# Output products of two attentions in one stream, and the query product taken ahead of its normalisation

## What is computed

```
h = rms_norm(x, norm_mix_g)
qa, ka, va, qb, kb, vb, ga, gb = split(h @ w_in)
ya = windowed_attention(qa, ka, va) @ w_oa      # 8 heads of 128
yb = dilated_attention(qb, kb, vb) @ w_ob       # 4 heads of 128
x  = x + (sigmoid(ga) * ya + sigmoid(gb) * yb) @ w_out
h  = rms_norm(x, norm_ffn_g)
q  = h @ peer_wq                                # 16 query parts of 128
top 16 of q . keys for each part, top 16 of the 256 sums, softmax -> gates of experts
x  = x + sum over experts of gate * gelu(h . u) * v
out = rms_norm(x, norm_final_g)
```

## Time and profile before

| | |
|---|---|
| median of 3 runs | 2307.59 us (2306.1 to 2307.99) |
| the profiled execution's own time | 2307.83 us |
| its span, first to last instruction | 2306.0 us |
| mean granted TensorE clock | 0.993 |
| PE busy | 2251.5 us, 98% |
| DVE busy | 1523.8 us, 66% |
| ACT busy | 1054.3 us, 46% |
| POOL busy | 177.3 us, 8% |

### The profile page before, as it was taken

How to read it: one execution, slowest core, us unless ns; L and a number is a source line. 1 busy time by engine, 2 the same in 40 slices (tenths; PEclk the granted TensorE clock), 3 DMA queues, 4 the chain that set the end, 5 groups by cost and what they waited for, 6 DMA issues and landing times.

```text
span 2306.0 us, 40258 instructions
## 1 busy us (share of the span) xinstructions
PE 2251.5 (98%) x12034; PEld 1930.6 (84%) x12034; DVE 1523.8 (66%) x2475; ACT 1054.3 (46%) x1541; POOL 177.3 (8%) x222
## 2 busy tenths in 40 slices
PE   7999999999898999999999999999999999999997
PEld 6888888888687888888888888888888888888885
DVE  6555566676567888878999999555555555555555
ACT  5444455446444444454444444444444444444443
POOL 0000000001302012221111111000000000000000
PEclk9999999999999999999999999999999999999999
DMA  6655544445454555554444444556555656555553
GB/s 223 227 186 183 181 164 156 154 144 204 137 190 171 169 179 182 182 182 164 159 160 162 164 160 159 185 187 215 195 191 192 192 195 212 191 191 193 194 195 137
DMA packets 114690, 415.56 MB, mean 180 GB/s; under 512 B 12974, under 2 KB 15662, under 8 KB 114022
## 3 DMA queue, kind: packets, MB, share of 16 engines
q1 hardware_dynamic: 114662, 415.23, 54.0%
HBM read 410.94 MB, written 4.24 MB: 180 GB/s over the span
## 4 chain that ended last, share of the span: by engine, by line
PE 95%; DVE 2%; ACT 1%; issue 1%; POOL 1%; DMA 0%; POOLq 0%; SPq 0%; DVEq 0%; ACTq 0%
PE ps L1251 40%; PE ps L1476 30%; PE ps L1254 20%; PE ps L1453 2%; PE ps L1362 1%; PE ps L1344 1%; POOL merged L456 1%; DVE lo L756 0%; DMA raw<-w_qk 0%; PE ps L1353 0%; PE ps L1422 0%; ACT hi L499 0%; ACT move L538 0%; DVE y L1238 0%; DVE work L774 0%
## 5 line engine op out<-in xcount | busy, mean ns | idle before, releaser
L1251 PE MATMUL ps<-move,hi 128*128 128x512 f32 x3840 | 1384.0, 403 | 31.2 <-DVE lo L756 18.5
L756 DVE TENSOR_TENSOR lo<-raw,hi 128x1024 fp32r<-128x1024 f32 x760 | 930.6, 1225 | 664.8 <-PE ps L1476 335.1
L1254 PE MATMUL ps<-move,lo 128*128 128x256 f32 x3840 | 1040.6, 281 | 0.0
L499 ACT CAST hi<-raw 128x1024 fp32r<-128x1024 f32 x760 | 791.3, 1047 | 201.4 <-DMA raw<-w_down 108.4
L1251 PEld LDWEIGHTS ps<-move,hi 128*128 128x128 f32 x3840 | 719.2, 189 | 190.5 <-DVE lo L756 17.3
L1254 PEld LDWEIGHTS ps<-move,lo 128*128 128x128 f32 x3840 | 729.4, 190 | 16.3
L507 ACT COPY upper<-ps 128x256 f32<-128x256 f32 x272 | 100.7, 373 | 645.5 <-PE ps L1251 645.3
L1476 PE MATMUL ps<-hi,act_hi 128*128 128x512 f32 x1024 | 315.5, 389 | 1.6 <-DVE lo L756 1.5
L1476 PE MATMUL ps<-lo,act_hi 128*128 128x512 f32 x1024 | 315.2, 389 | 0.0
L1476 PE MATMUL ps<-hi,act_lo 128*128 128x512 f32 x1024 | 315.2, 389 | 0.0
L1476 PEld LDWEIGHTS ps<-hi,act_hi 128*128 128x128 f32 x1024 | 192.0, 188 | 42.3 <-DVE lo L756 1.9
(11 more groups left out here) (162 smaller groups left out, 974.2 us busy)
## 6 DMA issues: line engine op xcount, KB each, us to landing
raw<-w_u SPq DMA_DIRECT2D x256, 512.0 KB, 3.3
raw<-w_down SPq DMA_DIRECT2D x256, 512.0 KB, 3.4
raw<-w_qk SPq DMA_DIRECT2D x68, 512.0 KB, 3.3
raw<-w_gate SPq DMA_DIRECT2D x64, 512.0 KB, 3.3
raw<-w_out SPq DMA_DIRECT2D x32, 512.0 KB, 3.3
raw<-w_pq SPq DMA_DIRECT2D x32, 512.0 KB, 3.6
raw<-w_v SPq DMA_DIRECT2D x28, 512.0 KB, 3.3
raw<-w_oa SPq DMA_DIRECT2D x16, 512.0 KB, 3.3
```

Of the source, the lines that this page charges most:

```text
L499: nc.scalar.copy(hi[slot][:], raw[slot][:]).then_inc(hi_ready, 1)
L756: nc.vector.tensor_tensor(lo[s % LOS][:], raw[s % RAW][:], hi[s % RAW][:].bitcast(F32), ALU.subtract).then_inc(lo_ready, 1)
L1251: return nc.tensor.matmul(ps[bank][:], hi[slot][:, col:col + P], m, start=first, stop=last)
L1254: return nc.tensor.matmul(ps[bank][:, 0:T], lo[lslot][:, col:col + P], m[:, 0:T], start=False, stop=False, skip_group_check=True)
```

## The change

oa and ob become one stage o of 24 chunks in the order a0 b0 a1, b1 a2 a3, b2 a4 a5, ... (`O_ORDER`; the weights are stacked so on the host). In o and pq every weight tile gets three products of 256 columns that accumulate in one place (`added`: high by high, low by high, high by low), so no halves are left to copy and add. DVE's `weigh` takes blocks from PSUM and multiplies by the gates; POOL has no part in it. In out, ACT and DVE also split g * x1, without rstd, into a new buffer `move2` (`keep_raw`, `split_raw`), from which pq is computed. The sum of squares, rstd, the 32 transposes and the split of the normalised h for u move in between pq's chunks (`squares_and_turns`, `norm2`, `root2`, `keep_h2`, `split_h2`, `turned`); POOL multiplies x1 by rstd into `xr` (four instructions of 1024 columns). Since scores now lack rstd, the exponential gets it as a factor per token (`rstd_tok`). ACT copies query blocks from PSUM. The copy of the turned x1 to memory is issued behind pq's loads, and POOL's fill of `act` waits for pq's last chunk. The buffer of turned x1 moves from 64 KB to 32 KB of the arena. The o loops and the pq loops are unrolled.

The diff, cut to what the text speaks of:

```diff
...
-CHUNKS = {"qk": 2 * N_QK, "v": 2 * N_V, "gate": 2 * N_GATE, "oa": KT, "ob": KT // 2,
+CHUNKS = {"qk": 2 * N_QK, "v": 2 * N_V, "gate": 2 * N_GATE, "o": KT + KT // 2,
           "out": 2 * KT, "pq": 2 * HC, "u": 2 * NK, "down": 2 * NK}
-BLOCKS = {"qk": N_QK, "v": N_V, "gate": N_GATE, "oa": KT, "ob": KT, "out": KT, "pq": HC, "u": NK}
+BLOCKS = {"qk": N_QK, "v": N_V, "gate": N_GATE, "o": KT, "out": KT, "pq": HC, "u": NK}
...
+UPPER0 = {"qk": 0, "out": BLOCK0["o"], "u": BLOCK0["o"] + KT}
...
-TURN_BANKS = (2, 3, 4, 6, 7)
+TURN_BANKS = (2, 3, 4)
...
+TURN0 = 2 * BODY
...
+O_ORDER = [("a", 0), ("b", 0), ("a", 1)]
+for _n in range(1, KT // 2):
+    O_ORDER += [("b", _n), ("a", 2 * _n), ("a", 2 * _n + 1)]
+O_DONE = [()] * len(O_ORDER)
+for _c, (_kind, _n) in enumerate(O_ORDER):
+    if _c == 1:
+        O_DONE[_c] = (0,)
+    elif _c > 1 and _kind == "a":
+        O_DONE[_c] = (_n,)
...
-        h2 = at("h2", ARENA + 48 * KB, [P, KT, T])
-        x1_nat = at("x1_nat", ARENA + 64 * KB, [P, TT, D])
+        move2 = at("move2", ARENA + 48 * KB, [P, KT, 2 * T], F32R)
+        xr = at("xr", ARENA, [P, KT, T])
+        x1_nat = at("x1_nat", ARENA + 32 * KB, [P, TT, D])
...
+        rstd_tok = at("rstd_tok", ARENA + 113 * KB + 64, [P, TT])
...
+            with sp.Fori(0, 2) as it:
+                for s in range(BODY):
+                    load("o", it, s)
+            sp.wait_ge(att_ready, 4)
+            sp.dma_start(x_again[:], A["x_t"]).then_inc(x_again_in, 16)
+            with sp.Fori(2, CHUNKS["o"] // BODY) as it:
+                for s in range(BODY):
+                    load("o", it, s)
...
-            sp.wait_ge(merged_lo, KT + 4)
+            sp.wait_ge(merged_lo, KT)
             sp.dma_start(keys_sb[:], A["keys"]).then_inc(keys_in, 16)
-            sp.wait_ge(x1_copied, 8)
-            sp.dma_start(x1_dram.ap(), x1_nat[:].rearrange("p a d -> p (a d)")).then_inc(x1_out, 16)
             with sp.Fori(1, CHUNKS["pq"] // BODY) as it:
                 for s in range(BODY):
                     load("pq", it, s)
+            sp.wait_ge(x1_copied, 8)
+            sp.dma_start(x1_dram.ap(), x1_nat[:].rearrange("p a d -> p (a d)")).then_inc(x1_out, 16)
...
-            pool.wait_ge(gated_a, KT + 2)
-            with pool.Fori(0, KT // 4) as it:
-                for e in range(4):
-                    n = it * 4 + e
-                    pool.wait_ge(block_summed, n + BLOCK0["ob"] + 3)
-                    pool.wait_ge(sig_ready, KT)
-                    nc.gpsimd.tensor_tensor(merged[e][:], merged[e][:], pick1(gates, n + KT), ALU.mult).then_inc(gated_b, 1)
-                    pool.wait_ge(gated_b, n + 1)
-                    nc.gpsimd.tensor_tensor(merged[e][:], merged[e][:], pick1(gates, n), ALU.add).then_inc(merged_ready, 1)
+            pool.wait_ge(x1_ready, KT)
             nc.gpsimd.iota(iota16[:], [[1, TOPK]], base=0, channel_multiplier=0,
                            allow_small_or_imprecise_dtypes=True).then_inc(iota_ready, 1)
-            pool.wait_ge(move_ready, 8)
+            pool.wait_ge(rstd_done, 1)
+            for q in range(4):
+                part = slice(4 * q, 4 * q + 4)
+                nc.gpsimd.tensor_tensor(xr[:, part, :], x1[:, part, :], rstd[:].unsqueeze(1).to_broadcast([P, 4, T]),
+                                        ALU.mult).then_inc(xr_ready, 1)
+            pool.wait_ge(xr_ready, 4)
+            pool.wait_ge(chunk_used, CHUNK0["u"] + RAW)
             pool.wait_ge(x1_out, 16)
...
+                    if name == "pq":
+                        if s % 2:
+                            n, e = it * 2 + s // 2, s // 2
+                            a.wait_ge(chunk_used, it * BODY + c0 + s + 1 + RAW)
+                            a.wait_ge(key_scores, n + 1)
+                            nc.scalar.copy(query[e][:], ps[e][:, 0:T]).then_inc(block_summed, 1)
...
+            def sigmoid_of(n):
+                a.wait_ge(block_summed, BLOCK0["gate"] + KT + n + 3)
+                both = gates[:].rearrange("p (k n) t -> p k n t", k=2)[:, :, n, :]
                 nc.scalar.activation(both, both, ACT.Sigmoid).then_inc(sig_ready, 1)
-            a.wait_ge(block_summed, BLOCK0["gate"] + KT + 2 + 2)
-            gate(0, -2)
-            gate(0, -1)
-            with a.Fori(0, CHUNKS["oa"] // BODY - 1) as it:
-                body("oa", it, gate)
-            body("oa", CHUNKS["oa"] // BODY - 1, lambda it, s: gate(it, s) if s < 2 else None)
-            def keep_merged(it, s):
-                for e in range(2):
-                    n = it * 8 + 2 * s + e
+            def keep_merged(c):
+                for n in O_DONE[c]:
                     a.wait_ge(merged_ready, n + 1)
-                    nc.scalar.copy(move[:, bass.ds(n, 1), 0:T].rearrange("p a t -> p (a t)"), merged[s % 2 * 2 + e][:]
-                                   ).then_inc(merged_hi, 1)
-            left = run(a, body, "ob", (keep_merged, 1), carry=True)
+                    nc.scalar.copy(move[:, n, 0:T], merged[n % 4][:]).then_inc(merged_hi, 1)
+            sigmoid_of(0)
+            sigmoid_of(1)
+            for c in range(CHUNKS["o"]):
+                hi_of(CHUNK0["o"], 0, c + 2)
+                if c + 2 < KT:
+                    sigmoid_of(c + 2)
+                if c >= 2:
+                    keep_merged(c - 2)
+            def last_merged(it, s):
+                keep_merged(CHUNKS["o"] - 2)
+                keep_merged(CHUNKS["o"] - 1)
+            left = [(last_merged, 1, 0)]
...
+            def keep_raw(it, s):
+                if s % 2:
+                    n = it * 2 + s // 2
+                    a.wait_ge(x1_ready, n + 1)
+                    nc.scalar.activation(move2[:, bass.ds(n, 1), 0:T].rearrange("p a t -> p (a t)"), pick1(x1, n), ACT.Copy,
+                                         scale=g_ffn[:, bass.ds(n, 1)]).then_inc(raw_hi, 1)
...
+            def root2(it, s):
+                if it == 0 and s == 2:
+                    nc.scalar.preload_act_table(ACT.Sqrt)
+                if it == 1 and s == 0:
+                    a.wait_ge(inv_ready, 2)
+                    nc.scalar.activation(rstd[:], work[:], ACT.Sqrt).then_inc(root_ready, 1)
+                if it == 2 and s == 2:
+                    a.wait_ge(rstd_turned, 1)
+                    nc.scalar.copy(rstd_tok[:], ps[5][:, 0:T].rearrange("p (t k) -> p t k", t=TT)[:, :, 0]).then_inc(rstd_kept, 1)
+            def keep_h2(it, s):
+                k = it * BODY + s - TURN0
+                if 0 <= k < KT:
+                    a.wait_ge(xr_ready, k // 4 + 1)
+                    nc.scalar.activation(move[:, k, 0:T], xr[:, k, :], ACT.Copy, scale=g_ffn[:, k:k + 1]).then_inc(h2_hi, 1)
...
+            for tt in range(TT):
+                nc.scalar.activation(found_g[:, tt, :], found_g[:, tt, :], ACT.Exp, scale=rstd_tok[:, tt:tt + 1]
+                                     ).then_inc(soft_ready, 1)
...
+            def weigh(c):
+                kind, i = O_ORDER[c]
+                v.wait_ge(chunk_used, CHUNK0["o"] + c + 1 + RAW)
+                if kind == "b":
+                    v.wait_ge(sig_ready, 2 * i + 2)
+                    for n in (2 * i, 2 * i + 1):
+                        nc.vector.tensor_tensor(gates[:, KT + n, :], ps[2 + n % 2][:, 0:T], gates[:, KT + n, :], ALU.mult
+                                                ).then_inc(gated_b, 1)
+                else:
+                    v.wait_ge(sig_ready, i + 1)
+                    nc.vector.tensor_tensor(merged[i % 4][:], ps[i % 2][:, 0:T], gates[:, i, :], ALU.mult
+                                            ).then_inc(block_summed, 1)
+                for n in O_DONE[c]:
+                    v.wait_ge(block_summed, BLOCK0["o"] + n + 3)
+                    v.wait_ge(gated_b, n + 1)
+                    nc.vector.tensor_tensor(merged[n % 4][:], merged[n % 4][:], gates[:, KT + n, :], ALU.add
+                                            ).then_inc(merged_ready, 1)
...
+            def split_merged(c):
+                for n in O_DONE[c]:
                     v.wait_ge(merged_hi, n + 1)
-                    nc.vector.tensor_tensor(move[:, bass.ds(n, 1), T:2 * T].rearrange("p a t -> p (a t)"),
-                                            merged[s % 2 * 2 + e][:],
-                                            move[:, bass.ds(n, 1), 0:T].rearrange("p a t -> p (a t)").bitcast(F32),
-                                            ALU.subtract).then_inc(merged_lo, 1)
-            left = run(v, body, "ob", (gate_b, 1), (split_b, 2), carried=left, carry=True)
+                    nc.vector.tensor_tensor(move[:, n, T:2 * T], merged[n % 4][:], move[:, n, 0:T].bitcast(F32), ALU.subtract
+                                            ).then_inc(merged_lo, 1)
+            for c in range(CHUNKS["o"]):
+                lo_of(CHUNK0["o"], 0, c + 1)
+                if c == 0:
+                    keep_gate(N_GATE // 2, -1)
+                    split_att(3)
+                if c >= 2:
+                    split_merged(c - 2)
```

(106 more changed lines are left out.)

169 lines of the change are left out of this document (41 added, 128 removed).

## The result

The changed kernel takes 2285.48 us (median of 4 runs, 2285.29 to 2286.26) against 2307.79 us (4 runs, 2306.1 to 2308.1): a ratio of 0.9906, interval 0.9892 to 0.992. Run again on another chip it gave 2284.67 us and 0.9902 (0.9885 to 0.9918). The gain is 22.3 us; 27.0 were forecast, with a range of 2274 to 2292 us.

A forecast was written before the change was run, and what follows sets the result against it. PE, busy for 98% of the span, was taken as the bound. Terms of 68.4 + 90.4 + 95.9 + 4.7 + 4.5 = 263.9 us replace 290.9, 27.0 less, so 2307.83 becomes 2280.8 us; range 2274 to 2292.

The forecast's parts named there:

- Rival B: Stream o waits on VectorE: 1.3 us at each of eight b-chunks, 10 us given back, 2291 us; chance 0.08.
- Rival A: VectorE bounds pq: eight blocks with splits each 0.8 us over, norm costing 8 us, 2290.7 us left; chance 0.15.
- Rival C: In `added`, weight loads bound narrow products: 0.57 us a tile instead of 0.353, kernel at 2378 us; chance 0.03.
- Rival D: No change in kernel time: several small delays together eat the 27 us; chance 0.03.
- Step (b): Three products of 256 columns instead of 512 + 256 per tile: zero, upper end 3 us, twice that for rounded rows.
- The start of o: First chunks of stream o: 0.7 us on top of 24 chunks at 2.82 us, 68.4 us in all.
- Step (g): In pq, norm and POOL's multiplications make VectorE late: 4.5 us; 1.1 without mutual hold-up, 8 if more is hit.
- 0.3 us for a slower clock: In pq, the clock may fall after the stall; most of that falls into VectorE's waits, so 0.3 us is added.
- (c): out starts without the 5.4 us wait and the slow clock behind it: 32 chunks at 2.83 us, 90.4 us.
- (d): Seam from out to pq: the last raw block is there at about 4.6 us, due at 5.2; zero wait.
- Step (f): In pq, 32 transposes with seams 3.9 us, product of ones 0.5, two transposes of rstd 0.3: 4.7 us.
- step (h): The rest: store of turned x1 zero, at most 3 us; moved fills of `act`; late-fetched unrolled code 0 to 3 us.

The follow-up runs named there:

- ahead of rankings: The changed kernel with each of GpSimd's four multiplications by rstd waiting for the count of a ranking's first step: 2285.5 us.
- inside rankings: The changed kernel with GpSimd's second to fourth multiplications by rstd started by a ranking's second step: 2281.39 us; with the root's last steps one chunk later 2281.17 us.
- small multiplications: The changed kernel with GpSimd's four multiplications by rstd of 1024 columns cut into sixteen of 256: 2281.32 us, ratio 0.9888.

## Why the prediction was right, point by point

**The direction and the mechanism held.** GpSimd no longer works beside VectorE in o, PE has no wait from 518 to 699 us, the sums are off the path, and the seams are closed: all as laid out. Rival B (waits in o) had none in the first execution; in other runs one `lo` in o came late by 0.19 us (the change's second execution) and by 0.35 (ahead of rankings), so the stream has little room there. Rival A (VectorE bounds pq in every block) did not come: PE is busy for 65.00 of the 65 us from 720 to 785, with VectorE at 55.6. Rival C would have made a tile 0.57 us; it is 0.360. Rival D is ruled out by the interval.

**The miss is 4.7 us** by the median, and 4.9 by the profiled execution (2285.66 against 2280.8), against which the sum was made: 3.1 in the stretch, 1.5 ahead of it, 0.2 around the span. Its terms:

- Step (b), three products of 256 columns, was taken at zero, with 3 us as the upper end and 6 as the outermost. This is the term that was mis-sized: it measured 4.3 us. In o 576 products take 69.17 us instead of 67.7, 1.5 more. In pq 14 blocks at 6.20 instead of 6.03 us are 2.4 more, and the four chunks ahead of the first key product take 11.5 instead of 11.1. The row that it went by the earlier trace rows already read 0.12 us a product against 0.118, but at a resolution of 0.01 us. And the pair's 0.353 us, from oa and out, was set against narrow products in pq too, where the pair is quicker: (6.03 - 0.44)/16 = 0.349 a tile against 0.360. The run with narrow products everywhere shows the same 6.20, so it is the products, not the seams. The start of o, put at 0.7 us more than the pace, took 0.2.
- Step (g), the stall, was put at 4.5 us and measured 4.2 and 3.9 against the run without the multiplication; as what is left of pq beside chunks, key products and transposes, it is 4.5 in the first execution. The place, the eighth chunk's 2.8 us and the tenth chunk's 1.1 us (2.73 and 0.86) were right, and so was the 2.4 us for a free multiplication (2.38 to 2.41 inside rankings). That VectorE and GpSimd hold each other up for a whole instruction was the branch that decided: 1.1 us had been written for the case without it, and 1.4 us are left where nothing is multiplied. In the traces a split that takes 0.48 us was held until the multiplication ended at 710.67, and a ranking beside one stayed at 3.09 us. The Trainium skill, page "SBUF — State Buffer", section "SBUF: two separate sides", says that GpSimd's instruction and a VectorE operation with two SBUF inputs exclude each other for the whole instruction; the traces agree. The 0.3 us for a slower clock fits too: 4.2 us where it fell, 3.9 where it did not.
- Steps (c) and (d), out and its seams, were right: 90.4 us, and no wait. Step (f), the transposes and the small products in pq, was put at 4.7 us and took 4.1: 8 x 0.43, 0.43 for the product of ones and 0.22 for the transposes of rstd. It left no wait, and neither did step (h): the unrolled code, the store of x1 and the fills of `act` cost nothing that a row shows.
- 1.46 us were in no step: o begins later than in the profile of before, though nothing ahead of it changed. The windows of 48 to 52 us, before and after:

```profile
48.00:52.00 4.00, 4.00 (x25) 3.48 (x24) 1.99 (x3) 2.20 (x3) 0.00 (x0) 0.98 0.47 140
```

```profile
48.00:52.00 4.00, 4.00 (x15) 3.44 (x14) 1.11 (x1) 1.03 (x2) 0.00 (x0) 0.55 0.44 133
```

Ahead of these windows, in both, PE waits 3.24 us until 45.3 us, and the granted clock from 44 to 48 us is 0.59. Then it is back at 0.98 in one execution and still near its lower level, 1.2 GHz, in the other (0.55). In the run inside rankings it was 1.00 from 44 to 52 us, behind the same wait of 3.24 us, and o began at 516.08. Over ten profiled executions of the change and its variants o began between 516.1 and 518.6 us; the change's own second execution had 516.88. The second execution of the same kernel shows that this is scatter between executions, and it is why o to u is the better measure. It was no part of the forecast, and it could as well have fallen the other way.

Sum: 4.3 us of pace, less 0.5 at the start of o and 0.6 in (f), with the stall at its 4.5, make 267.0 for 263.9 but for 0.1. So the total is nearer than its largest error, because two small terms had been put too high. With the start of o the spans differ by 22.4 us where 27.0 stood.

## What to carry to other kernels

A helper engine's instruction costs by what it overlaps, not by its length: short pieces, or a start inside a stretch where the neighbour reads one tensor, made the same multiplications free or nearly so (out to u 194.8 and 195.2 us, against 194.8 without them). Check the start in the trace, because a count given by a sequencer can come while the instruction ahead of it still runs. When a change turns few wide products into many narrow ones, price them from a long piece of the chain (576 products in one row), where 7 ns show, and not from single rows of two digits, and take the pace of before from the same stage: here a tile of before was 0.353 us in out and 0.349 in pq.

## What the runs showed that was not expected

- The price of a product is not its columns alone. In the last stage, where all have 512 columns, the chain has 2207 products in one piece of 500.25 us, 0.2267 each; all-narrow streams take 0.1201, and a wide and a narrow one together 0.3533 in out, 6.5 ns more than 0.2267 + 0.1201. So two narrow ones cost 13.5 ns more than a wide one, and splitting the wide one of a mixed tile cost 7 by the pace of out and 10.6 in pq. Why the mixed tile's pace differs by stage is open.
- A wait of 2.7 us on PE was followed by a granted clock of 0.83 over ten microseconds in one execution, and by 1.00 in another of the same kernel. After waits of 1.4 to 1.7 us in pq, in every run above, it stayed at 1.00.
- Moving the root's last steps one chunk later took its wait from 1.4 to 0.2 us, yet together with the small multiplications it lost 0.9 us of o to u against those alone.
